# Hybrid decoder layer on one Trainium2 core: another order of three engines' queues around a seven-product output projection

## The chip, the cores and the metric

The kernel is written in Bass and runs on 1 core of one Trainium2 chip, in one launch. The metric is the device time in microseconds (us). A profile is one execution of the program recorded by the hardware profiler; its own time and its span stand beside each other below.

## What is computed

One layer of a hybrid decoder for 512 tokens of width 1024, all in float32. A combined input projection feeds two token mixers (a gated linear recurrence and a top-k sparse attention). Each mixer's output is projected up to width 1024, the two are weighted by sigmoid gates and added (`merged`). What the change touches is the end:

```python
merged = jax.nn.sigmoid(ga) * ua + jax.nn.sigmoid(gb) * ub      # (512, 1024)
y = jnp.einsum('bld,de->ble', merged, w_out)                    # (512, 1024) x (1024, 1024)
return layer_norm(ALPHA * x + y, ln_g, ln_b)                    # over the 1024 columns of a row
```

## The kernel before, in words

**Every float32 product is three products.** ACT rounds an operand to a high part (`hi`), POOL or DVE subtracts to get the low part (`lo = raw - hi`), and PE adds hi*hi, hi*lo and lo*hi into one PSUM bank. The input projection and the two up projections run as 31 "units" of weights (`UNITS`, 256 columns each), each in 4 quarters, so there are 124 steps `q`. SP loads the units, ACT makes their high parts, POOL their low parts, PE multiplies. Beside that the mixers' work is placed by hand: each engine has a function `side(q)`, and tables such as `OUT_HI_AT`, `OUT_LO_AT` and `T1_AT` say at which q an engine does what. A step q is only a place in an engine's queue, each engine runs its queue strictly in order, and semaphores tie the engines together.

**The up projections** are the last four units, `up0` to `up3`, q = 108 to 123: 16 fills of a bank with 12 matmuls each (`quarter_up`), over four banks. `merge(m)` on DVE, m = 0 to 7 (before line L1719), reads two fills, frees their banks with its first two instructions (L1711, L1712), adds them to `mix` (L1715), and after ACT has rounded it (`round_merged`, L1196) subtracts the low part (L1718), which is what PE needs as operand m of the output projection. After an odd m, `sum_rows` (L1728 to L1735) makes four sums and differences, `round_sums` (ACT, L1201) and `sum_rows_lo` (DVE, L1741) their high and low parts. The last merge (m = 7) and what follows it stand behind the loop over q.

**The output projection** multiplies a 2x2 block matrix (halves of the 512 rows; even and odd tiles of 128 of the inner dimension against halves of the columns) with seven products of half-size blocks in place of eight (a Strassen-like scheme). PE takes them in the order `OUT_WEIGHTS` = b11, b21, t1, t2, b22, t3, t4, and each for i = 0 and 1 (128 rows each), 12 matmuls of 128x128 by 128x512 for each of these 14: 168 matmuls (L958, L960, L961). Sums: b11 and b21 give the rows 0 to 255, columns 0 to 511 (bank `c11`). b11 alone is also kept aside by ACT (`keep_first`, L1222, into `first_sum`), because b21 is added into the same bank: b21 waits for `first_kept`. The common sum U = b11 + t2 goes into the three other blocks. The weights b11, b12, b21, b22 come from HBM; t1 to t4 are their differences, made by DVE (`sum_out`, L1762, 128x2048 elements each; t1 at q = `T1_AT`). Their high parts are made by ACT (`split_out_hi`, L1217, two halves each), their low parts by POOL (`split_out_lo`, L2044, four pieces each, in the order 0, 1, 4, 3, 5, 6 of `OUT_WEIGHTS`), that of t1 by DVE (`first_sum_lo`, L1768).

**Behind the last merge** ACT's queue before is: the last `round_merged`, the last `round_sums`, a load of the table of functions (L1346), the two halves of `split_out_hi(4)`, `keep_first` for i = 0 and 1, the splits 3, 5, 6, then the layer norm's small steps. DVE's queue is: last merge, `sum_rows`, t2, `sum_rows_lo`, t3, `rows_11(0)`, t4, `rows_11(1)`, `rows_12` for both i, `late_residuals` for both i, statistics of b22's rows, `rows_22` for both i, statistics of t4's rows. In `rows_12` (L1793 to L1795) DVE makes U (`u_sum`) and V = c12 + U (`v_sum`) in SBUF and puts V plus ALPHA*x back into bank `c12`, on which b22 is added by PE (wait on `pre_12`). `late_residuals` (L1779 by way of `with_residual`) adds ALPHA*x of the rows 256 to 511 to U and V in SBUF. `rows_22` (L1808, L1809) combines them with t3 and frees t4 (`pre_21`):

```python
def rows_22(i):
    t = 2 + i
    wait_y_full(dve, "t3", i)
    nc.vector.tensor_tensor(y_sb[:, t, 512:], c21_bank[i][:], y_sb[:, t, 512:], ALU.add).then_inc(dve_step, 1)
    nc.vector.tensor_tensor(c21_bank[i][:], c21_bank[i][:], y_sb[:, t, 0:512], ALU.add).then_inc(pre_21, 1)
```

**The layer norm** works on 4 tiles of 128 rows (t) in two halves of 512 columns. DVE takes statistics (L1771) and aggregates (L1774); ACT takes the root (`root`). The scaling is done in one of two ways: on DVE with two instructions (`normalise_half`, L1819, L1822), or on ACT and POOL (`shift` and `scale_rows` on ACT, then `scale_columns` with two instructions on POOL, L2050, L2052). `ON_POOL` lists for each t the halves that take the second way: before it is both halves of t = 0 and 1, and half 1 of t = 2, five in all. SP stores each half in the order of t as soon as it is done (L626).

Of the kernel before, what the change touches and what calls it, by code (L numbers as in the profile page):

```python
# [29 lines left out]
ALU = mybir.AluOpType  # L30
# [64 lines left out]
OUT_HI_AT = {110: (0, 0), 111: (0, 1), 118: (1, 0), 119: (1, 1), 121: (2, 0), 122: (2, 1)}  # L95
OUT_LO_AT = {110: ((0, 0),), 111: ((0, 1),), 114: ((0, 2),), 115: ((0, 3),), 118: ((1, 0),), 119: ((1, 1),),
             120: ((1, 2),), 121: ((1, 3),)}
T1_AT = 116
ON_POOL = ((0, 1), (0, 1), (1,), ())
# [16 lines left out]
def hybrid_kernel(nc, x_t, x_tok, w_units, w_kiwi, b_cols, b_ia, b_vb, lb_cols, g_cols, rel_bias,  # L116
                  ln_g, ln_b, one_hot, ident, causal, tree_masks, out):
    with ExitStack() as ctx:
# [75 lines left out]
        with ExitStack() as s:  # L194
# [13 lines left out]
            with ExitStack() as s2:  # L208
                v_sum = sb("v_sum", [P, 2, SEQ], stack=s2)
# [92 lines left out]
        first_kept, pre_12, pre_21 = sem("first_kept"), sem("pre_12"), sem("pre_21")  # L302
        y_full, y_aggr = sem("y_full"), sem("y_aggr")
# [211 lines left out]
        def row_source(t, half):  # L515

            if half == 1 and t < 2:
                return c12_bank[t][:]
            if half == 0 and t >= 2:
                return c21_bank[t - 2][:]  # L520
            return y_sb[:, t, half * 512:half * 512 + 512]
# [109 lines left out]
        def _(pe):  # L631
# [302 lines left out]
            for n, i in OUT_ORDER:  # L934
                name = OUT_WEIGHTS[n]
                bank, (b_hi, b_lo) = out_banks[name][i], out_weights(n)
                first = name in ("b11", "t1", "t2", "t3")
# [4 lines left out]
                elif name == "t1":  # L942
                    pe.wait_ge(proj_out[i], NPROJ[NMAIN])
                elif name in ("t2", "t3"):
                    pe.wait_ge(up_out[i + 2 * (name == "t3")], 2 * KT // 4)
                elif name == "b22":
                    pe.wait_ge(pre_12, i + 1)
                else:
                    pe.wait_ge(pre_21, i + 1)
# [17 lines left out]
        def _(act):  # L967
# [255 lines left out]

            def root(t):
# [5 lines left out]

            def shift(t):
# [3 lines left out]
                act.wait_ge(ln_shift, 2 * t + 1)  # L1235
                nc.scalar.activation(rstd[:, t, 3:4], rstd[:, t, 2:3], ACT.Copy,
                                     scale=rstd[:, t, 1:2]).then_inc(ln_shift, 1)
                act.wait_ge(ln_shift, 2 * t + 2)
# [63 lines left out]
            for q in range(4 * NMAIN):  # L1302
# [13 lines left out]
                if q in OUT_HI_AT:  # L1316
                    split_out_hi(*OUT_HI_AT[q])
# [22 lines left out]
                if m is not None:  # L1340
                    round_merged(m)
                    if m % 2:
                        round_sums(m // 2)
            round_merged(KT - 1)
            round_sums(PAIRS - 1)
            nc.scalar.preload_act_table_set("natural_log_exp_and_others")  # L1346
            for half in range(2):
                split_out_hi(4, half)
            for i in range(2):
                keep_first(i)  # L1350
            for n in (3, 5, 6):
                for half in range(2):
                    split_out_hi(n, half)
            for t in range(TB):
                root(t)
                if t < TB - 1:
# [6 lines left out]
        def _(dve):  # L1363
# [412 lines left out]
            def with_residual(t, half, other):  # L1776

                c = slice(half * 512, half * 512 + 512)
                link(nc.vector.scalar_tensor_tensor(out=y_sb[:, t, c], in0=y_sb[:, t, c], scalar=ALPHA, in1=other,  # L1779
                                                    op0=ALU.mult, op1=ALU.add))  # L1780

            def rows_11(i):
# [3 lines left out]
                with_residual(i, 0, c11_bank[i][:])  # L1786
                row_stats(i, 0)

            def rows_12(i):
# [3 lines left out]
                link(nc.vector.tensor_tensor(u_sum[:, i, :], m6_bank[i][:], first_sum[:, i, :], ALU.add))  # L1793
                link(nc.vector.tensor_tensor(v_sum[:, i, :], c12_bank[i][:], u_sum[:, i, :], ALU.add))
                nc.vector.scalar_tensor_tensor(out=c12_bank[i][:], in0=y_sb[:, i, 512:], scalar=ALPHA,  # L1795
                                               in1=v_sum[:, i, :], op0=ALU.mult, op1=ALU.add).then_inc(pre_12, 1)

            def late_residuals(i):

                dve.wait_ge(res_in[2 + i], 16)  # L1800
                with_residual(2 + i, 0, u_sum[:, i, :])
# [333 lines left out]
```

## Time and profile before

| what | value |
|---|---|
| median of 3 runs | 476.32 us (475.74 to 476.94) |
| the profiled execution, its own time | 476.05 us |
| its span | 474.2 us |
| PE busy | 448.2 us, 95% of the span |
| DVE, ACT, POOL busy | 320.1, 237.7, 194.8 us |
| mean granted clock of PE | 0.976 |

The span is what the trace covers; 1.85 us of the execution's own time lie around it. Engines are PE (matmul), PEld (its weight loads), DVE, ACT, POOL and SP (which issues the DMAs). A row of a timeline gives start and duration in us, the engine, the line of the kernel, the operation, output<-inputs with their sizes, how many are merged into the row, and in brackets how long the engine was idle before it and who ended that. In the rows, high parts of the b weights are `x_hi`, `w_hi` or `w_late`, low parts `x_lo` or `w_lo`, as they lie in buffers that are used again; `z_a`, `z_b` and `w_raw` hold the raw weights.

### The profile page before, as it was taken

What the parts mean: (1) busy time and instruction counts of PE and PEld (TensorE: products, weight loads), DVE (VectorE), ACT (ScalarE), POOL (GpSimd) and SP (SyncE); (2) the same over time, 40 slices, a digit from 0 to 9 for tenths busy, and PEclk for the clock granted to TensorE, in tenths of its full rate; (3) what the DMA queues carried; (4) which work ended last, traced back from release to release, by engine and by line L of the source; (5) the groups of instructions that cost most, each with busy time, mean ns of one, the idle gap of its engine ahead of it and who ended that gap; (6) DMA issues with size and microseconds to landing.
All of it is one profiled execution on the core that took longest, in us unless ns stands there. A gap on an engine that the chain in (4) does not pass through costs nothing.

```text
span 474.2 us, 7699 instructions
## 1 busy us (share of the span) xinstructions
PE 448.2 (95%) x2946; PEld 364.9 (77%) x2946; DVE 320.1 (68%) x581; ACT 237.7 (50%) x401; POOL 194.8 (41%) x179
## 2 busy tenths in 40 slices
PE   8999999999999999999999999999999998929990
PEld 7778888888888788888878878878888876717770
DVE  4535699999999643458899958806300678895685
ACT  5734554442457625658685658347743224345050
POOL 0444444490667607540040000000655775409956
PEclk9999999999999999999999999999999998978996
DMA  8818202274026600222202220320464520420003
GB/s 260 276 42 311 75 25 83 92 183 169 0 91 156 201 1 2 88 90 88 91 2 91 91 90 1 107 74 1 140 219 173 177 89 4 171 91 1 0 27 151
DMA packets 16724, 47.73 MB, mean 101 GB/s; under 512 B 2440, under 2 KB 4272, under 8 KB 16176
## 3 DMA queue, kind: packets, MB, share of 16 engines
q1 hardware_dynamic: 16448, 47.05, 30.0%
q8 instruction: 23, 0.38, 0.3%
q10 hardware_dynamic: 240, 0.20, 0.2%
q14 instruction: 13, 0.11, 0.1%
HBM read 43.04 MB, written 2.11 MB: 95 GB/s over the span
## 4 chain that ended last, share of the span: by engine, by line
PE 82%; DVE 7%; POOL 4%; ACT 3%; issue 2%; DMA 1%; POOLq 0%; DVEq 0%; ACTq 0%
PE bank L633 20%; PE bank L634 20%; PE bank L635 20%; PE bank L794 2%; PE bank L779 2%; PE bank L877 2%; PE bank L830 2%; POOL y_sb L2050 1%; PE bank L958 1%; PE bank L960 1%; PE bank L961 1%; POOL y_sb L2052 1%; PE bank L770 1%; PE bank L769 1%; DVE y_sb L1779 1%
## 5 line engine op out<-in xcount | busy, mean ns | idle before, releaser
L1970 POOL TENSOR_TENSOR w_lo<-w_raw,w_hi 128x512 fp32r<-128x512 f32 x84 | 112.7, 1368 | 161.8 <-ACT w_hi L969 161.8
L633 PE MATMUL bank<-x_hi,w_hi 128*128 128x512 f32 x336 | 133.0, 396 | 0.0
L634 PE MATMUL bank<-x_lo,w_hi 128*128 128x512 f32 x336 | 131.2, 390 | 0.0
L635 PE MATMUL bank<-x_hi,w_lo 128*128 128x512 f32 x336 | 130.9, 390 | 0.0
L633 PEld LDWEIGHTS bank<-x_hi,w_hi 128*128 128x128 f32 x336 | 63.1, 188 | 13.8 <-issue 0.8
L635 PEld LDWEIGHTS bank<-x_hi,w_lo 128*128 128x128 f32 x336 | 63.1, 188 | 13.6
L634 PEld LDWEIGHTS bank<-x_lo,w_hi 128*128 128x128 f32 x336 | 63.1, 188 | 12.2
L969 ACT ACTIVATE w_hi<-w_raw 128x1024 fp32r<-128x1024 f32 (+2 forms) x63 | 62.4, 1011 | 5.8 <-PE bank L635 3.3
L1056 ACT ACTIVATE prob<-prob,nmax 128x128 f32<-128x128 f32 (+3 forms) x32 | 17.7, 555 | 41.6 <-DVE nmax L1497 41.5
L633 PE MATMUL bank<-o_hi,w_hi 128*128 128x512 f32 x64 | 25.5, 399 | 2.3 <-DVE mix L1711 2.3
L1473 DVE MAX8 best<-score 128x8 f32<-128x256 f32 (+2 forms) x48 | 26.8, 558 | 1.0
L1485 DVE COPY prob_t<-bank 128x128 f32<-128x128 f32 (+3 forms) x32 | 14.3, 486 | 19.0 <-PE bank L779 18.9
L1474 DVE MATCH_REPLACE8 score<-best,score 128x256 f32<-128x256 f32 (+2 forms) x48 | 26.0, 542 | 0.0
L634 PE MATMUL bank<-o_lo,w_hi 128*128 128x512 f32 x64 | 25.6, 400 | 0.0
L635 PE MATMUL bank<-o_hi,w_lo 128*128 128x512 f32 x64 | 25.6, 400 | 0.0
L633 PE MATMUL bank<-w_hi,x_hi 128*128 128x512 f32 x64 | 25.3, 395 | 0.0
L635 PE MATMUL bank<-w_hi,x_lo 128*128 128x512 f32 x64 | 25.0, 390 | 0.0
L634 PE MATMUL bank<-w_lo,x_hi 128*128 128x512 f32 x64 | 24.9, 390 | 0.0
L1711 DVE TENSOR_TENSOR mix<-bank,gate_a_hi 128x512 f32<-128x512 f32 x4 | 2.7, 686 | 31.7 <-PE bank L635 31.7
L1988 POOL TENSOR_TENSOR logit<-t,pen 128x256 f32<-128x256 f32 x24 | 17.4, 738 | 9.1 <-DVE nmax L1497 9.1
L1046 ACT ACTIVATE relus<-bank 128x256 f32<-128x256 f32 (+2 forms) x24 | 10.5, 489 | 21.0 <-PE bank L759 21.0
L1463 DVE SCALAR_TENSOR_TENSOR score<-relus,w_idx,score 128x256 f32<-128x256 f32 (+2 forms) x21 | 15.6, 744 | 7.7 <-ACT relus L1046 6.0
(274 smaller groups left out, 855.4 us busy)
## 6 DMA issues: line engine op xcount, KB each, us to landing
w_raw<-in_w_units SPq DMA_DIRECT2D x58, 512.0 KB, 4.7
w_raw<-in_w_units SPq DMA_DIRECT2D x2, 1024.0 KB, 4.8
y_sb<-in_x_tok SPq DMA_DIRECT2D x4, 512.0 KB, 5.2
out<-y_sb SPq DMA_DIRECT2D x8, 256.0 KB, 2.0
x_raw_hi<-in_x_t SPq DMA_DIRECT2D x4, 256.0 KB, 4.7
x_raw_lo<-in_x_t SPq DMA_DIRECT2D x4, 256.0 KB, 6.6
t_turned<-t_row SPq DMA_DIRECT2D x1, 1024.0 KB, 9.6
q_hi_g<-q_hi_g SPq DMA_DIRECT2D x8, 128.0 KB, 4.0
```

The source lines that it names most:

```text
L633: nc.tensor.matmul(dst, a_hi, b_hi, start=first, stop=False)
L634: nc.tensor.matmul(dst, a_hi, b_lo, start=False, stop=False)
L635: return nc.tensor.matmul(dst, a_lo, b_hi, start=False, stop=last)
L969: nc.scalar.activation(split_target(u, kiwi_hi, x_hi, w_hi)[:, k, :], raw(u)[:, k, :], ACT.Copy).then_inc(done, 1)
L1046: nc.scalar.activation(relus[:, i % 2, 0:n], log_bank[i % 2][:, 0:n], ACT.Relu, scale=QSCALE).then_inc(log_out[i % 2], 1)
L1056: nc.scalar.activation(prob[:, i % 4, 0:n], prob[:, i % 4, 0:n], ACT.Exp, bias=nmax[:, i % 4:i % 4 + 1], scale=-1.0, accum_out=prob_sum[:, ...
L1463: ins = nc.vector.scalar_tensor_tensor(out=score[b][:], in0=relus[:, i % 2, 0:n], scalar=w, in1=score[b][:], op0=ALU.mult, op1=ALU.add)
L1473: link(nc.vector.max(best8[:], score[b][:]))
L1474: link(nc.vector.match_replace(score[b][:], best8[:], score[b][:], TAKEN))
L1485: nc.vector.tensor_copy(prob_t[:, i % 4, 0:n], turn_bank[i % 2][:, 0:n]).then_inc(turn_out[i % 2], 1)
L1970: nc.gpsimd.tensor_tensor(split_target(u, kiwi_lo, x_lo, w_lo)[:, k, :], raw(u)[:, k, :], split_target(u, kiwi_hi, x_hi, w_hi)[:, k, :].bi ...
L1988: nc.gpsimd.tensor_tensor(logit[:, i % 2, n - band:n], t5[:, h, 2 * P - band:], pen[b][:, n - band:] if b else causal_sb[:], ALU.add).then ...
```

## The change

ACT's and POOL's work on the weights b11, b21, t1 moves to other steps, t1 itself one step earlier; the table load moves from behind the last `round_sums` to q = 109; `split_out_hi(4)` goes ahead of the last `round_merged`, and `keep_first` right behind `round_merged` and `round_sums`. DVE adds ALPHA*x to bank `c12` before t2 is done (`early_rows`), and U by one instruction afterwards; `v_sum` and `late_residuals` go. ACT copies U into bank `c21` (`move_u`), t3 is added onto it by PE. Rows stay in their PSUM banks up to the normalisation's second instruction. `ON_POOL` has two halves left in place of five; DVE takes six in place of three.

```diff
--- before.py
+++ after.py
@@ -92,11 +92,10 @@
 LO_DVE = tuple(range(Q_PREP[0] // 4 + 1, Q_MERGE // 4 + 2))
-OUT_HI_AT = {110: (0, 0), 111: (0, 1), 118: (1, 0), 119: (1, 1), 121: (2, 0), 122: (2, 1)}
-OUT_LO_AT = {110: ((0, 0),), 111: ((0, 1),), 114: ((0, 2),), 115: ((0, 3),), 118: ((1, 0),), 119: ((1, 1),),
-             120: ((1, 2),), 121: ((1, 3),)}
-T1_AT = 116
-ON_POOL = ((0, 1), (0, 1), (1,), ())
+OUT_HI_AT = {109: ((0, 0),), 110: ((0, 1),), 117: ((1, 0),), 118: ((1, 1),), 120: ((2, 0), (2, 1))}
+OUT_LO_AT = {110: 0, 119: 1}
+T1_AT, T1_LO_AT = 115, 121
+ON_POOL = ((), (1,), (1,), ())
 ROUNDS = TOPK // 8
@@ -300,6 +297,7 @@
         first_kept, pre_12, pre_21 = sem("first_kept"), sem("pre_12"), sem("pre_21")
+        u_done, u_moved, early_12 = sem("u_done"), sem("u_moved"), sem("early_12")
         y_full, y_aggr = sem("y_full"), sem("y_aggr")
@@ -514,11 +512,7 @@
-            if half == 1 and t < 2:
-                return c12_bank[t][:]
-            if half == 0 and t >= 2:
-                return c21_bank[t - 2][:]
-            return y_sb[:, t, half * 512:half * 512 + 512]
+            return ((c11_bank, c12_bank), (c21_bank, m6_bank))[t // 2][half][t % 2][:]
@@ -934,15 +928,17 @@
                 bank, (b_hi, b_lo) = out_banks[name][i], out_weights(n)
-                first = name in ("b11", "t1", "t2", "t3")
+                first = name in ("b11", "t1", "t2")
                 if name == "b11":
...
                     pe.wait_ge(proj_out[i], NPROJ[NMAIN])
-                elif name in ("t2", "t3"):
-                    pe.wait_ge(up_out[i + 2 * (name == "t3")], 2 * KT // 4)
+                elif name == "t2":
+                    pe.wait_ge(up_out[i], 2 * KT // 4)
+                elif name == "t3":
+                    pe.wait_ge(u_moved, i + 1)
                 elif name == "b22":
@@ -1221,6 +1217,12 @@
+            def move_u(i):
+
+                act.wait_ge(up_out[2 + i], 2 * KT // 4)
+                act.wait_ge(u_done, i + 1)
+                nc.scalar.activation(c21_bank[i][:], u_sum[:, i, :], ACT.Copy).then_inc(u_moved, 1)
+
             def root(t):
@@ -1228,14 +1230,17 @@
+            def shifted(t):
+                return sum(bool(halves) for halves in ON_POOL[:t])
+
             def shift(t):
...
                 act.wait_ge(ln_rstd, t + 1)
-                act.wait_ge(ln_shift, 2 * t + 1)
+                act.wait_ge(ln_shift, 2 * shifted(t) + 1)
                 nc.scalar.activation(rstd[:, t, 3:4], rstd[:, t, 2:3], ACT.Copy,
                                      scale=rstd[:, t, 1:2]).then_inc(ln_shift, 1)
-                act.wait_ge(ln_shift, 2 * t + 2)
+                act.wait_ge(ln_shift, 2 * shifted(t) + 2)
@@ -1313,8 +1318,10 @@
                         split_hi(v, q - hi_quarter(v))
-                if q in OUT_HI_AT:
-                    split_out_hi(*OUT_HI_AT[q])
+                for n, half in OUT_HI_AT.get(q, ()):
+                    split_out_hi(n, half)
+                if q == 109:
+                    nc.scalar.preload_act_table_set("natural_log_exp_and_others")
                 if q == Q_ITEM[0] - 2:
@@ -1341,19 +1348,20 @@
                         round_sums(m // 2)
+            split_out_hi(4, 0)
+            split_out_hi(4, 1)
             round_merged(KT - 1)
+            keep_first(0)
             round_sums(PAIRS - 1)
-            nc.scalar.preload_act_table_set("natural_log_exp_and_others")
-            for half in range(2):
-                split_out_hi(4, half)
-            for i in range(2):
-                keep_first(i)
+            keep_first(1)
             for n in (3, 5, 6):
...
                     split_out_hi(n, half)
+            for i in range(2):
+                move_u(i)
             for t in range(TB):
                 root(t)
-                if t < TB - 1:
+                if ON_POOL[t]:
                     shift(t)
@@ -1773,54 +1781,59 @@
-            def with_residual(t, half, other):
+            def with_residual(dst, t, half, other):
                 c = slice(half * 512, half * 512 + 512)
-                link(nc.vector.scalar_tensor_tensor(out=y_sb[:, t, c], in0=y_sb[:, t, c], scalar=ALPHA, in1=other,
-                                                    op0=ALU.mult, op1=ALU.add))
+                return nc.vector.scalar_tensor_tensor(out=dst, in0=y_sb[:, t, c], scalar=ALPHA, in1=other,
+                                                      op0=ALU.mult, op1=ALU.add)
...
                 dve.wait_ge(res_in[i], 16)
-                with_residual(i, 0, c11_bank[i][:])
+                link(with_residual(c11_bank[i][:], i, 0, c11_bank[i][:]))
                 row_stats(i, 0)
+
+            def early_rows(i):
+
+                wait_y_full(dve, "t1", i)
+                dve.wait_ge(res_in[2 + i], 16)
+                link(with_residual(y_sb[:, 2 + i, 512:], 2 + i, 1, c12_bank[i][:]))
+                with_residual(c12_bank[i][:], i, 1, c12_bank[i][:]).then_inc(early_12, 1)
...
                 dve.wait_ge(first_kept, i + 1)
-                link(nc.vector.tensor_tensor(u_sum[:, i, :], m6_bank[i][:], first_sum[:, i, :], ALU.add))
-                link(nc.vector.tensor_tensor(v_sum[:, i, :], c12_bank[i][:], u_sum[:, i, :], ALU.add))
-                nc.vector.scalar_tensor_tensor(out=c12_bank[i][:], in0=y_sb[:, i, 512:], scalar=ALPHA,
-                                               in1=v_sum[:, i, :], op0=ALU.mult, op1=ALU.add).then_inc(pre_12, 1)
-
-            def late_residuals(i):
-
-                dve.wait_ge(res_in[2 + i], 16)
-                with_residual(2 + i, 0, u_sum[:, i, :])
-                with_residual(2 + i, 1, v_sum[:, i, :])
+                nc.vector.tensor_tensor(u_sum[:, i, :], m6_bank[i][:], first_sum[:, i, :], ALU.add).then_inc(u_done, 1)
+                dve.wait_ge(u_done, i + 1)
+                dve.wait_ge(early_12, i + 1)
+                nc.vector.tensor_tensor(c12_bank[i][:], c12_bank[i][:], u_sum[:, i, :], ALU.add).then_inc(pre_12, 1)
...
                 wait_y_full(dve, "t3", i)
-                nc.vector.tensor_tensor(y_sb[:, t, 512:], c21_bank[i][:], y_sb[:, t, 512:], ALU.add).then_inc(dve_step, 1)
-                nc.vector.tensor_tensor(c21_bank[i][:], c21_bank[i][:], y_sb[:, t, 0:512], ALU.add).then_inc(pre_21, 1)
-                steps[0] += 1
-                dve.wait_ge(dve_step, steps[0])
+                link(nc.vector.tensor_tensor(m6_bank[i][:], c21_bank[i][:], y_sb[:, t, 512:], ALU.add))
+                with_residual(c21_bank[i][:], t, 0, c21_bank[i][:]).then_inc(pre_21, 1)
                 row_stats(t, 1)
...
                 c = slice(half * 512, half * 512 + 512)
-                y = y_sb[:, t, c]
+                y = row_source(t, half)
                 dve.wait_ge(y_aggr, t + 1)
-                link(nc.vector.scalar_tensor_tensor(out=y, in0=row_source(t, half), scalar=aggr[:, t, 0:1],
+                link(nc.vector.scalar_tensor_tensor(out=y, in0=y, scalar=aggr[:, t, 0:1],
                                                     in1=ln_gb[:, 0, c], op0=ALU.subtract, op1=ALU.mult))
                 dve.wait_ge(ln_rstd, t + 1)
-                nc.vector.scalar_tensor_tensor(out=y, in0=y, scalar=rstd[:, t, 1:2], in1=ln_gb[:, 1, c],
+                nc.vector.scalar_tensor_tensor(out=y_sb[:, t, c], in0=y, scalar=rstd[:, t, 1:2], in1=ln_gb[:, 1, c],
                                                op0=ALU.mult, op1=ALU.add).then_inc(y_done[t][half], 1)
+
+            def normalise(t):
+
+                for half in range(2):
+                    if half not in ON_POOL[t]:
+                        normalise_half(t, half)
@@ -1902,7 +1915,7 @@
                         sum_rows_lo(m // 2 - 1)
-                if q == T1_AT + 6:
+                if q == T1_LO_AT:
                     first_sum_lo()
@@ -1935,23 +1948,24 @@
             rows_11(1)
+            early_rows(0)
+            early_rows(1)
             rows_12(0)
             rows_12(1)
-            late_residuals(0)
-            late_residuals(1)
             for t in range(2):
...
                 aggregate(t)
+                if t == 0:
+                    normalise(0)
             rows_22(0)
             rows_22(1)
+            normalise(1)
             for t in (2, 3):
...
                 aggregate(t)
-                for half in range(2):
-                    if half not in ON_POOL[t]:
-                        normalise_half(t, half)
+                normalise(t)
@@ -2053,8 +2067,9 @@
                 side(q)
-                for n, piece in OUT_LO_AT.get(q, ()):
-                    split_out_lo(n, piece)
+                if q in OUT_LO_AT:
+                    for piece in range(4):
+                        split_out_lo(OUT_LO_AT[q], piece)
             for n in LO_ORDER[2:]:
```

## Rows read from the trace of the kernel before

**Rows 1.** The page: PE's busy time, and the chain that ended last, by engine

```profile
PE 448.2 (95%) x2946; PEld 364.9 (77%) x2946; DVE 320.1 (68%) x581; ACT 237.7 (50%) x401; POOL 194.8 (41%) x179
PE 82%; DVE 7%; POOL 4%; ACT 3%; issue 2%; DMA 1%; POOLq 0%; DVEq 0%; ACTq 0%
```

**Rows 2.** Windows of PE: length, busy (matmuls), granted clock, DMA share, GB/s

```profile
392.90:396.60 3.70, 3.69 (x9) 0.55 0.02 4
413.10:414.10 1.00, 0.08 (x1) 1.00 1.02 401
427.10:430.80 3.70, 3.62 (x9) 0.50 0.00 0
```

**Rows 3.** Timeline of PE, last third of the up projections and the output projection

```profile
392.91 0.53 PE L633 MATMUL bank<-o_hi,w_hi 128*128 128x512 f32 x1 [2.28 <-DVE mix L1711]
396.66 0.39 PE L633 MATMUL bank<-o_hi,w_hi 128*128 128x512 f32 x1
...
410.98 0.39 PE L958 MATMUL bank<-x_hi,even_hi 128*128 128x512 f32 x1
...
414.11 0.50 PE L958 MATMUL bank<-x_hi,even_hi 128*128 128x512 f32 x1 [0.93 <-DVE even_lo L1718]
...
427.18 0.80 PE L958 MATMUL bank<-x_hi,odd_hi 128*128 128x512 f32 x1 [9.35 <-ACT first_sum L1222]
...
451.16 0.39 PE L958 MATMUL bank<-x_hi,s_hi_hi 128*128 128x512 f32 x1
...
461.81 0.39 PE L961 MATMUL bank<-x_hi,odd_lo 128*128 128x512 f32 x1
```

**Rows 4.** Timeline of ACT around the up projections' start and the last merge

```profile
372.05 0.42 ACT L1196 ACTIVATE even_hi<-mix 128x256 fp32r<-128x256 f32 x1 [5.05 <-DVE mix L1715]
...
419.43 0.63 ACT L1196 ACTIVATE odd_hi<-mix 128x512 fp32r<-128x512 f32 x1 [5.82 <-DVE mix L1715]
...
423.35 1.28 ACT L1346 ACT_TABLE_LOAD   x1
424.64 2.00 ACT L1217 ACTIVATE w_late<-w_raw 128x1024 fp32r<-128x1024 f32 x2
426.55 1.06 ACT L1222 ACTIVATE first_sum<-bank 128x512 f32<-128x512 f32 x2
```

**Rows 5.** Timeline of DVE over the same stretch and the tail

```profile
389.36 2.90 DVE L1762 TENSOR_TENSOR z_a<-z_b,z_a 128x2048 f32<-128x2048 f32 x1 [2.89 <-POOL x_lo L2044]
392.18 0.68 DVE L1711 TENSOR_TENSOR mix<-bank,gate_a_hi 128x512 f32<-128x512 f32 x1
...
413.63 0.42 DVE L1718 TENSOR_TENSOR even_lo<-mix,even_hi 128x256 fp32r<-128x256 f32 x1 [1.33 <-ACT even_hi L1196]
...
415.11 2.28 DVE L1768 TENSOR_TENSOR w_lo<-z_a,w_hi 128x2048 fp32r<-128x2048 f32 x1
...
433.40 2.67 DVE L1762 TENSOR_TENSOR w_raw<-w_raw,z_a 128x2048 f32<-128x2048 f32 x1
435.99 0.68 DVE L1779 SCALAR_TENSOR_TENSOR y_sb<-y_sb,bank 128x512 f32<-128x512 f32 x1
...
446.94 1.30 DVE L1795 SCALAR_TENSOR_TENSOR bank<-y_sb,v_sum 128x512 f32<-128x512 f32 x1
448.15 1.77 DVE L1779 SCALAR_TENSOR_TENSOR y_sb<-y_sb,u_sum 128x512 f32<-128x512 f32 x1
...
453.12 0.70 DVE L1771 BATCH_NORM_STATS2 stats<-bank 128x6 f32<-128x512 f32 x1
...
460.57 0.75 DVE L1819 SCALAR_TENSOR_TENSOR y_sb<-bank,aggr,ln_gb 128x512 f32<-128x512 f32 x1
```

**Rows 6.** Timeline of POOL: a split beside DVE's wide subtraction, the last scaling

```profile
432.63 7.10 POOL L2044 TENSOR_TENSOR w_lo<-z_a,w_hi 128x512 fp32r<-128x512 f32 x4
...
468.92 1.59 POOL L2052 TENSOR_TENSOR y_sb<-y_sb,ln_gb 128x512 f32<-128x512 f32 x1
```

**Rows 7.** The store DMAs: issues (duration ns min/median/max, first and last start us)

```profile
L626 SPq DMA_DIRECT2D out<-y_sb x8: 332/341/454, 458.8 to 471.4; - x8
```

More of the change, by code:

```diff
@@ L207, in hybrid_kernel @@
             g_b_1 = sb("g_b_1", [P, 4, SEQ], stack=s)
-            with ExitStack() as s2:
-                v_sum = sb("v_sum", [P, 2, SEQ], stack=s2)
             mix = sb("mix", [P, 2, SEQ], stack=s)
```

## The prediction

> **What bounds the kernel now.** I read the page first: PE is busy for 95% of the span and is 82% of the chain that ended last, and the chain leaves PE only near the end [rows 1]. So what counts is where PE stands still and what lies behind its last product. The timeline of PE gives three gaps in the stretch that the change touches, each with its releaser, and a tail [rows 3]. PE waits 2.28 us before 392.91 for DVE's third merge; 0.93 us before 414.11 for the low part of operand 6; 9.35 us before 427.18 for ACT's copy `first_sum`. Its last product starts at 461.81 and takes 0.39, so it ends at 462.2, and the span ends at 474.2: a tail of 12.0 us without PE. The windows add a cost that a gap has behind it: after the gap of 2.28 and after that of 9.35 the granted clock is 0.55 and 0.50, the lower of the two levels (1.2 GHz), for nine matmuls each; around the gap of 0.93 it stays at 1.00 (2.4 GHz) [rows 2]. The pace at the higher level is (461.81 - 451.16)/47 = 0.227 us a matmul; the nine slow ones took 396.66 - 392.91 = 3.75 instead of 2.04, so one fall of the clock costs 1.7 us [rows 3].
>
> **Term 1: t1 and the gap of 2.28.** DVE stood idle for 2.89 us before t1 (389.36) until POOL had b11's last low parts [rows 5]. These now come at q = 110, right behind up1's part; t1 moves one step earlier in DVE's queue, with the same neighbours. So t1 can start at 389.36 - 2.89 = 386.5. It costs 2.28 (the subtraction of that width with POOL idle) to 2.90 (beside POOL) [rows 5]. POOL is released at about the same moment for up3, so I take nearly the upper end: the third merge starts at 389.3 instead of 392.18. It frees PE's bank 0.7 later, at 390.0, before PE wants it (392.91 - 2.28 = 390.6). The gap and its slow matmuls go; the 72 matmuls left of the up projections end at 390.5 + 72 x 0.227 = 406.8, against 410.98 [rows 3]: 4.2 us earlier.
> The trace shows the same width at 2.28 and 2.90, and a 128x512 operation with two SBUF inputs at 1.77 beside POOL [rows 5]. The Trainium skill (SBUF - State Buffer, "Who interferes with whom") says that a VectorE instruction with two SBUF inputs and a GpSimd one that reads SBUF exclude each other, the first to start holding the port throughout. By that rule with t1 first, merge 3 comes 0.6 us sooner and the total is 461.6; with POOL first it is what I take.
>
> **Term 2: that gain is mostly not PE's.** From merge 3 to the low part of operand 6 DVE's chain took 413.63 + 0.42 - 392.18 = 21.9 us [rows 5]. The change adds to it: ACT does both halves of b21's high part ahead of operand 4 instead of one (+1.0, half of the 2.00 for two [rows 4]); `first_sum_lo`, 2.2 us [rows 5], now stands ahead of merge 6 instead of behind. It saves 0.7 of the 1.33 that DVE waited for operand 6 [rows 5], since t1's high parts no longer stand ahead of that rounding (0.42 remain, plus a hand-over). Sum 24.4: operand 6 is ready at 389.3 + 24.4 = 413.7, against 414.05. PE reaches it at 406.8 + 9 x 0.227 = 408.9, about 0.6 later if merge 5 (12 us behind merge 3) frees its bank late. So b11 gets **a new gap of 4 to 5 us**, longer than the one with a clock fall [rows 2, 3], and I charge 1.7: b11's other 15 matmuls end at 413.7 + 3.4 + 1.7 = 418.8.
>
> **Term 3: the gap of 9.35.** It was ACT's queue: rounding of operand 7 at 419.43, sums, table load 1.28, two splits 2.00, then the copies [rows 4]. Now the splits are ahead of the rounding (they need b22 and up3's end, both past by 413.7), the table load is at q = 109, where ACT idles 5.05 us before 372.05 [rows 4] and hides 1.28 and the moved first half of b11 (1.0); without that cover it would cost 1.3. Operand 7 follows operand 6 by 3.9 us (s_lo 1.1, merge and rounding 2.8, as from 417.3 to 420.06), the copy takes 0.55 (1.06 for two): first copy at 418.1, before b11 ends. The second stands behind `round_sums`, at 420.9; b21's second half wants it at 418.8 + 2.7 = 421.5. No wait: b21 starts at 418.8 instead of 427.18.
>
> **Term 4: from b21 to the end of PE.** Before it took 462.2 - 427.18 = 35.0, with one clock fall: 33.3 without. Can the others follow? DVE's queue from its last sums (419.7): t2 2.2, low part 1.1, t3 2.2, rows_11 1.4, t4 2.67, rows_11 1.4, early_rows 2 x 1.4, U and its addition 1.4, by 0.68 for each add, 0.70 for each statistic and 2.28 to 2.67 for the wide ones [rows 5]: 434.9, up to 1.2 later beside POOL. PE is there at 418.8 + 6 x 2.72 = 435.1. Wait of 0 to 0.9 at b22; I take 0.3. `move_u` (0.55 each) runs on an idle ACT about 4 us before t3; `rows_22` needs 1.4 per i and has 2.7. POOL: b22's low parts 414.5 to 421.6, t2's from 423.2 (its high part) to 430.3 by the slow 7.10 for four [rows 6]; PE wants the last at 431.8. Covered by 1.5. PE ends at 418.8 + 33.3 + 0.3 = 452.4: **9.8 us earlier**.
>
> **Term 5: the tail.** Before, POOL's backlog of ten scalings ended at 470.51 [rows 6] and the last store was issued at 471.4 [rows 7], 2.8 before the span's end. Now tile 0 is normalised under t3, tile 1 and half of tile 2 under t4, and DVE, 0.7 late at the last product, does statistics 0.7, aggregate 0.2, and four instructions of at most 0.75 plus 0.04 between them [rows 5] = 3.2: 4.8 behind PE; with the store's 2.8 the tail is 7.6 instead of 12.0: **4.4 us less**. ACT's and POOL's half of tile 2 ends about 1 us before that. No store but the last is on the path.
> The second normalising instruction with a bank as input isn't in the trace: 0.75 (its neighbour [rows 5]) at the low end, 1.30 (two SBUF inputs, a bank as output, beside POOL [rows 5]) at the high end. It has one SBUF input like the 0.75, so I take that.
> The add with a bank as input took 0.68 [rows 5]. The Trainium skill (VectorE: DVE Perf Modes, "The TRN2 errata") speaks against this change here: 120 + FD cycles from PSUM, 58 + FD from SBUF, which is 65 ns more for each of the operations that now stay in banks. By that rule the tail's four would add 0.3 us (462.5); the row shows no such surplus.
>
> **Sum.** 474.2 - 9.8 - 4.4 = 460.0 span, plus the 1.85 around it = 461.9 for an execution like the profiled one (476.05), which lies 0.3 under the median of the runs: 462.2.
>
> **Rivals.**
> (a) The sum above, 460.5 to 464: chance 0.60.
> (b) DVE becomes the bound: operations that write or read banks cost 1.30 instead of 0.68 to 0.75. Five of them lie between t4 and b22 (+2.8, less the 0.2 of slack), four in the tail (+2.2): +4.8, 467.0, or 465.5 with half in the first part. For it the 1.30 row; against it that the same form beside an idle POOL is never so slow. 0.14.
> (c) Less is lost in front: no clock fall behind b11's gap, or t1 first and less contention. Then b11 ends 1.7 sooner but waits 1.0 for the copy; with merge 3 at 388.7 all of it 0.6 sooner: 460.3 to 461.5. 0.13.
> (d) POOL's low parts of t2 arrive after PE wants them, since DVE's wide subtractions now run beside them. If both fours cost 2 us more than 7.1: +2.5, 464.7. 0.08.
> (e) Slower: the clock. PE comes out of b11's new gap at the lower level and stays there. Ahead of it are 15 + 144 = 159 matmuls at 0.2 more each. Nine are charged; the gain of 14.1 is gone once 70 more are slow, and if all 150 are, the time is 462.2 + 30 = 492. Against it, both falls in the trace ended after nine matmuls [rows 2]. 0.03.
> (f) The change doesn't do what it says: ACT, now with b22's split ahead of operand 7's rounding, stands at the load of b22, everything behind it waits, and b21 starts as late as before; some 10 us come back, and with (b) in the tail nothing is left: 475. The load would have to land 13 us late. 0.02.
>
> A measurement of this kernel can tell 0.3%, 1.4 us, from no change. (a) to (d) are faster by more, 0.95; (f) is the same, 0.02; (e) slower, 0.03. The range holds (a), (c), most of (b) and (d): 459.8 to 466.
>
> **What would show it.** Right: no gap before fill 10; a gap of 4 to 5 us inside b11 released by DVE `even_lo`, with a window at half clock behind it; b21 starts about 419 with no `first_sum` gap; PE ends at 452 and the span about 7.6 later, the last instruction being DVE's. Wrong: a gap at b21 or over 1 us at b22 or t2; statistics or normalising instructions over 1 us; t1 still waiting for POOL; a slow window longer than 4 us.

## The result, and the profile after

The changed kernel takes 463.86 us (463.53 to 463.86, 4 runs), the one before 476.22 us (475.74 to 476.94): a ratio of 0.9737, 95% interval 0.9721 to 0.9754, 12.4 us less. The forecast was 462.2, in a range of 459.8 to 466. In the profiled execution the span is 461.9 us against 474.2. Times of the experiments below are medians of 4 or 5 runs, each with the ratio to the kernel before on the same chip. The variant that came out fastest had one execution of 2539 us among its five: its ratio leaves that one out, its median of 461.18 does not (the other four have 460.97), and the cause was not looked for.

The timeline of PE after the change, every gap in the stretch (they answer to [rows 3]) and its last product:

```profile
403.04 0.50 PE L627 MATMUL bank<-o_hi,w_hi 128*128 128x512 f32 x1 [0.85 <-DVE mix L1719]
413.65 0.80 PE L954 MATMUL bank<-x_hi,even_hi 128*128 128x512 f32 x1 [2.83 <-DVE even_lo L1726]
423.54 0.50 PE L954 MATMUL bank<-x_hi,odd_hi 128*128 128x512 f32 x1 [0.62 <-ACT first_sum L1218]
434.47 0.50 PE L954 MATMUL bank<-w_hi,s_hi_lo 128*128 128x512 f32 x1 [0.27 <-POOL w_lo L2058]
454.10 0.39 PE L957 MATMUL bank<-x_hi,odd_lo 128*128 128x512 f32 x1
```

The gaps of 2.28 and 9.35 us are gone; four small ones, 4.6 us in all, stand for 12.6. PE ends at 454.5 instead of 462.2, and the tail behind it is 461.9 - 454.5 = 7.4 instead of 12.0. So of the 12.3 us of span, 7.7 came ahead of PE's end and 4.6 behind it. (This execution runs 0.43 behind that of before already at merge 0, DVE's first `mix` at 369.34 against 368.91, well ahead of anything that moved; differences below are given with that in mind, and it is called the offset.)

ACT around the last merge (to be read against [rows 4]):

```profile
417.69 0.63 ACT L1192 ACTIVATE odd_hi<-mix 128x512 fp32r<-128x512 f32 x1 [2.66 <-DVE mix L1723]
418.23 0.58 ACT L1218 ACTIVATE first_sum<-bank 128x512 f32<-128x512 f32 x1
421.94 1.06 ACT L1197 ACTIVATE s_hi_lo<-s_raw 128x1024 fp32r<-128x1024 f32 x1 [3.13 <-DVE s_raw L1743]
422.91 0.58 ACT L1218 ACTIVATE first_sum<-bank 128x512 f32<-128x512 f32 x1
```

The first copy of b11 follows the rounding at once; the second one waits 3.13 us for DVE's sums, and b21's second half waits for it. DVE after the change (against [rows 5]):

```profile
386.98 3.37 DVE L1770 TENSOR_TENSOR z_a<-z_b,z_a 128x2048 f32<-128x2048 f32 x1
390.27 0.68 DVE L1719 TENSOR_TENSOR mix<-bank,gate_a_hi 128x512 f32<-128x512 f32 x1
...
413.17 0.43 DVE L1726 TENSOR_TENSOR even_lo<-mix,even_hi 128x256 fp32r<-128x256 f32 x1 [0.48 <-ACT even_hi L1192]
...
416.03 1.63 DVE L1723 TENSOR_TENSOR mix<-mix,g_b 128x512 f32<-128x512 f32 x1
418.36 0.99 DVE L1726 TENSOR_TENSOR odd_lo<-mix,odd_hi 128x512 fp32r<-128x512 f32 x1 [0.70 <-ACT odd_hi L1192]
419.27 1.50 DVE L1736 TENSOR_TENSOR s_raw<-mix 128x256 f32<-128x256 f32 x1
...
456.08 0.76 DVE L1826 SCALAR_TENSOR_TENSOR bank<-bank,aggr,ln_gb 128x512 f32<-128x512 f32 x1
...
458.33 0.75 DVE L1829 SCALAR_TENSOR_TENSOR y_sb<-bank,rstd,ln_gb 128x512 f32<-128x512 f32 x1
```

and POOL (against [rows 6]):

```profile
414.16 6.33 POOL L2058 TENSOR_TENSOR w_late<-w_raw,w_late 128x512 fp32r<-128x512 f32 x4 [7.68 <-ACT w_late L1213]
425.29 9.13 POOL L2058 TENSOR_TENSOR w_lo<-z_a,w_hi 128x512 fp32r<-128x512 f32 x4 [4.79 <-ACT w_hi L1213]
434.38 5.03 POOL L2058 TENSOR_TENSOR x_lo<-z_b,x_hi 128x512 fp32r<-128x512 f32 x4
```

The reader is to see three things. In DVE's last merge and the first sum behind it the forms with two SBUF inputs take 1.63, 0.99 and 1.50 us where they take 0.69, 0.69 and 0.42 alone, and that is the stretch 414.2 to 420.5 in which POOL, which idled there before, makes b22's low parts. POOL's four pieces of t2 take 9.13 us, those of t3 5.03. And the normalising instructions with a bank as input take 0.75.

### The profile page after: what moved, and what is told of

It is laid out like the page before. It is cut to its first block, busy times and chain, and to the rows that moved or that the text cites. A ratio compares the mean times of both kernels' runs of the same rounds, so it can differ in the third digit from the quotient of the medians.

```text
span 461.9 us, 7700 instructions
## 1 busy us (share of the span) xinstructions
PE 448.9 (97%) x2946; PEld 365.5 (79%) x2946; DVE 319.4 (69%) x585; ACT 236.7 (51%) x398; POOL 185.3 (40%) x173
## 4 chain that ended last, share of the span: by engine, by line
PE 84%; DVE 9%; POOL 2%; issue 2%; ACT 2%; DVEq 0%; POOLq 0%
PE bank L627 21%; PE bank L628 21%; PE bank L629 20%; PE bank L788 2%; PE bank L773 2%; POOL w_lo L2058 2%; PE bank L871 2%; PE bank L824 2%; DVE s_lo L1749 1%; DVE z_a L1770 1%; DVE mix L1723 1%; PE bank L764 1%; PE bank L763 1%; PE bank L954 1%; PE bank L957 1%
```

## The experiments

**ACT's last part alone, on the kernel before.**

```diff
+                if q == 109:
+                    nc.scalar.preload_act_table_set("natural_log_exp_and_others")
...
+            split_out_hi(4, 0)
+            split_out_hi(4, 1)
             round_merged(KT - 1)
+            keep_first(0)
             round_sums(PAIRS - 1)
-            nc.scalar.preload_act_table_set("natural_log_exp_and_others")
-            for half in range(2):
-                split_out_hi(4, half)
-            for i in range(2):
-                keep_first(i)
+            keep_first(1)
```

> The kernel before with ACT's last part alone changed (table load at q = 109, b22's split ahead of the last rounding, the copies of b11 right behind the rounding and the sums). Theory (the gap of 9.35 us was ACT's order): the first copy ends near 420.6 instead of 427.1, b21 starts 6.6 us earlier, with a gap of about 2.9 us and one fall of the clock as before; tail of 12 us unchanged: 469.7 us. Rival (DVE's and POOL's backlog takes the place of ACT's): b21 starts early, but PE waits at t2 or b22, and less than 3 us come out: over 473 us.

Measured: 473.41 us, ratio 0.9942 (0.9927 to 0.9957): 2.8 us, not 6.6. The timelines of PE, DVE and POOL say where the rest stayed:

```profile
423.15 0.53 PE L958 MATMUL bank<-x_hi,odd_hi 128*128 128x512 f32 x1 [4.79 <-ACT first_sum L1222]
```

```profile
415.67 3.38 DVE L1769 TENSOR_TENSOR w_lo<-z_a,w_hi 128x2048 fp32r<-128x2048 f32 x1
420.35 1.60 DVE L1716 TENSOR_TENSOR mix<-mix,g_b 128x512 f32<-128x512 f32 x1
```

```profile
415.18 7.90 POOL L2045 TENSOR_TENSOR w_late<-w_raw,w_late 128x512 fp32r<-128x512 f32 x4 [5.72 <-ACT w_late L1217]
```

ACT was ready, but operand 7's rounding began at 421.99 instead of 419.43 (0.56 of it the offset of this execution), because the early split let POOL begin beside DVE's last wide subtraction (3.38 instead of 2.28) and merge (1.60 instead of 0.69). The rival's number held, not its mechanism: PE's small waits at b22 and t4 are 0.59 and 0.26. The tail was not unchanged either: PE ends at 459.40 in a span of 472.1, so it is 12.7 us.

**The same part undone, on the changed kernel** (order of ACT's queue: rounding, sums, b22's split, both copies; the table load stays at q = 109).

> The changed kernel with the two copies of b11 and b22's split put back behind the last sums on ACT; everything else as changed. Theory: b21's first half starts near 425.5 instead of 420.0, and a second fall of the clock costs 1.7 to 3: 471 to 473 us. Rival (b21's start does not decide, the low parts of t2 on POOL do): under 467 us.

Measured: 466.81 us, ratio 0.9807 (0.9790 to 0.9823), 3 us over the changed kernel; both theories missed (471 to 473, under 467 for the wrong reason).

```profile
422.35 0.79 PE L954 MATMUL bank<-x_hi,odd_hi 128*128 128x512 f32 x1 [5.75 <-ACT first_sum L1218]
```

```profile
415.29 0.69 DVE L1723 TENSOR_TENSOR mix<-mix,g_b 128x512 f32<-128x512 f32 x1
```

b21 starts at 422.35, not 425.5. With b22's split late, POOL idles until 420.95 and DVE's last merge runs at its own pace (0.69): the same coupling from the other side. The run takes back two things at once (the copies and b22's split), so the 3 us are not the price of the copies alone. That gave theory C below.

**Five halves of rows on POOL, as before.** `ON_POOL = ((0, 1), (0, 1), (1,), ())`.

> The changed kernel with five halves of rows scaled on POOL as before, in place of two. Theory (the tail got shorter because the rows' other work on DVE is done ahead, so that POOL could start early anyway): POOL starts its ten operations near 444.4, when t4's low parts are done, ends about 457.8, DVE's last two halves end the kernel as now: 463 to 464 us. Rival (the tail's 4.6 us come from taking three halves off POOL): 467.5 to 468.5 us.

Measured: 462.55 us, ratio 0.9717 (0.9702 to 0.9731): not slower but 1 us faster than the change (463.55 us and 0.9732 when it was run again, below). The intervals of the two ratios overlap; what speaks for a difference is that all four runs here (462.46 to 462.89) lie under all four there (463.31 to 463.66, on another chip), and the tail in the profiles.

```profile
453.66 0.39 PE L957 MATMUL bank<-x_hi,odd_lo 128*128 128x512 f32 x1
```

```profile
443.90 1.31 POOL L2064 TENSOR_TENSOR y_sb<-y_sb,ln_gb 128x512 f32<-128x512 f32 x1
...
455.71 1.26 POOL L2066 TENSOR_TENSOR y_sb<-y_sb,ln_gb 128x512 f32<-128x512 f32 x1
```

POOL starts its scalings at 443.90, as soon as t4's low parts are made, where before it started at 456.09; it is done at 457.0, DVE at 458.1. The tail is 460.7 - 454.05 = 6.65 us, 0.8 shorter than the change's, since DVE is free when the last product ends. The edit changes nothing but `ON_POOL`, so taking halves off POOL did not shorten the tail.

**The steps of the weights' parts as before** (`OUT_HI_AT`, `OUT_LO_AT`, `T1_AT` as in the kernel before, `first_sum_lo` at q = 122).

> The changed kernel with the steps of b11's, b21's and t1's parts and of t1 itself as before. Theory A (moving them only moves PE's wait, the chain on DVE decides): the gap of 2.3 us in the up projections is back with its fall of the clock, the gap in b11 is 1 us again, and one of 2.9 us stands before b21; time within 1 us of the changed kernel, 463 to 465 us. Theory B (the steps are worth the 2.2 us by which operand 7 comes sooner and a fall of the clock): 466 to 468 us.

Measured: 466.78 us, ratio 0.9805 (0.9790 to 0.9819): theory B by the time, the steps are worth 3 us. What theory A said of the first gap came true in part: it is back, but no fall of the clock follows it in this profile, and the gap in b11 is 2.49 us, not 1.

```profile
392.79 0.50 PE L628 MATMUL bank<-o_hi,w_hi 128*128 128x512 f32 x1 [2.29 <-DVE mix L1720]
414.00 0.50 PE L955 MATMUL bank<-x_hi,even_hi 128*128 128x512 f32 x1 [2.49 <-DVE even_lo L1727]
422.48 0.80 PE L955 MATMUL bank<-x_hi,odd_hi 128*128 128x512 f32 x1 [4.79 <-ACT first_sum L1219]
```

With the offsets taken off, operand 6 is 0.9 us later than in the change (PE goes on at 414.00 against 413.65, in an execution that is 0.56 ahead at merge 0). The rest is lost behind it, on DVE:

```profile
414.99 3.38 DVE L1777 TENSOR_TENSOR w_lo<-z_a,w_hi 128x2048 fp32r<-128x2048 f32 x1
419.68 1.60 DVE L1724 TENSOR_TENSOR mix<-mix,g_b 128x512 f32<-128x512 f32 x1
```

`first_sum_lo` stands ahead of merge 7 again, beside POOL's parts of b22 (414.51 to 422.41). The old steps with b22's parts moved away were not run, so how much of the 3 us is the order and how much the meeting with POOL is not shown.

**The change again, and three edits beside it.** In the first edit POOL makes b22's low parts behind t2's:

```diff
-        LO_ORDER = (0, 1, 4, 3, 5, 6)
+        LO_ORDER = (0, 1, 3, 4, 5, 6)
```

In the second PE gets twelve products more (`FILL = 12`) ahead of b11's last pair, so that it works through the gap:

```diff
+                        if name == "b11" and j == 3:
+                            pe.wait_ge(proj_out[0], NPROJ[NMAIN])
+                            for _ in range(FILL):
+                                nc.tensor.matmul(c12_bank[0][:], a_hi, b_hi[:, 2, :], start=True, stop=True)
```

The third is everything on the rows alone: the changed kernel with steps, ACT's last part, table load and `ON_POOL` as before.

> The changed kernel once more, beside the next three on one chip: 463.9 us by either theory, within 0.5.

> The changed kernel with one edit: POOL makes b22's low parts behind t2's instead of ahead of them. Theory C (the early split of b22 put POOL's work beside DVE's last merge, whose operations with two SBUF inputs then took 1.0 to 1.6 us instead of 0.4 to 0.7; that is why b11's second copy came at 423.5 and not at 421): DVE's last merge and sums take 2.3 us less, b21's second half starts 2 us sooner, POOL starts t2's low parts 2 us sooner, 461.9 us. Rival (DVE's pace there does not set PE's, or b22's low parts come too late): 463.5 us or more.

> The changed kernel with twelve products more (into a bank not yet in use, thrown away) ahead of b11's last pair, so that PE works through most of the gap. Theory C: the fall of the clock goes, b11 ends up to 3 us sooner, but b21's second half waits for ACT's second copy as before: 463.9 us, within 0.5. Rival (the fall of the clock, three us in this profile, is what made my forecast too low): 461 to 462 us.

> Everything of the change on the rows alone (early residuals, U copied into c21, rows kept in their banks, the normalisation of tiles 0 and 1 ahead of t3's and t4's rows), with the steps, ACT's last part, the table load and the halves on POOL as before. If the parts add up, the steps being worth 2.9 and ACT's part 3.0 and the halves on POOL -1.3: 468.5 us. If ACT's part and the steps each pay only with the other (two gaps in a row on one chain): 466 or 471 us. The tail by this theory is as in the run with five halves on POOL, 6.7 us behind PE's last product.

| kernel | us | ratio (interval) |
|---|---|---|
| the change again | 463.55 | 0.9732 (0.9719 to 0.9745) |
| b22's low parts behind t2's | 461.18 | 0.9679 (0.9666 to 0.9692) |
| gap in b11 filled | 463.32 | 0.9729 (0.9716 to 0.9742) |
| the rows' part alone | 470.40 | 0.9875 (0.9859 to 0.9890) |

The first edit bears theory C out: 2.4 us less than the change by the medians (2.6 without the long execution), 2.0 expected. ACT, DVE and POOL of that kernel:

```profile
419.69 0.58 ACT L1218 ACTIVATE first_sum<-bank 128x512 f32<-128x512 f32 x1
```

```profile
415.15 0.69 DVE L1723 TENSOR_TENSOR mix<-mix,g_b 128x512 f32<-128x512 f32 x1
416.54 0.69 DVE L1726 TENSOR_TENSOR odd_lo<-mix,odd_hi 128x512 fp32r<-128x512 f32 x1 [0.69 <-ACT odd_hi L1192]
417.14 0.42 DVE L1736 TENSOR_TENSOR s_raw<-mix 128x256 f32<-128x256 f32 x1
```

```profile
422.07 9.15 POOL L2058 TENSOR_TENSOR w_lo<-z_a,w_hi 128x512 fp32r<-128x512 f32 x4 [16.48 <-ACT w_hi L1213]
431.18 5.05 POOL L2058 TENSOR_TENSOR w_late<-w_raw,w_late 128x512 fp32r<-128x512 f32 x4
```

The second copy starts at 419.69 instead of 422.91 (0.9 of which is this execution's own lead), b21 doesn't wait for it at all, and PE ends at 451.3. PE's last product:

```profile
450.91 0.39 PE L957 MATMUL bank<-x_hi,odd_lo 128*128 128x512 f32 x1
```

The filled gap was to show what the fall of the clock costs. The windows of PE over the gap, filled (first) and in the change run again (second):

```profile
410.20:413.20 3.00, 2.92 (x13) 1.00 1.01 385
```

```profile
410.50:413.30 2.80, 0.00 (x0) 1.00 0.93 334
413.30:418.50 5.20, 3.70 (x15) 1.00 0.42 161
```

The time did not move. It could hardly have: the clock did not fall in the change run again either, after the same gap of 2.83 us (the granted clock is 1.00 behind it), while in the first profile of the change 14 matmuls behind that gap are at the lower level and in the run with five halves on POOL eight. So the filled gap says nothing of the fall's price. The two profiles of the same kernel do. Their spans are 461.9 with the fall and 461.6 without, but the one with the fall was already 0.35 late at merge 0 and behind the gap (413.65 against 413.30), and it is 0.33 late when PE ends (454.49 against 454.16): the fall took nothing. Without it b11 ends sooner, and PE waits 1.53 and 1.65 us for ACT's two copies instead of 0 and 0.62.

The rows' part alone brings 6.0 us, the largest share; the 468.5 us of parts that add up was 2 too low, and the 471 of parts that pay only together is nearer. PE's end is that of before (462.6 against 462.2), the tail 469.2 - 462.6 = 6.6 us:

```profile
462.23 0.39 PE L958 MATMUL bank<-x_hi,odd_lo 128*128 128x512 f32 x1
```

```profile
452.00 1.29 POOL L2064 TENSOR_TENSOR y_sb<-y_sb,ln_gb 128x512 f32<-128x512 f32 x1 [2.26 <-ACT y_sb L1249]
```

POOL starts at 452.0 for 456.09, because DVE takes the statistics of b22's rows when they are there, and not behind four late residuals [rows 5]. A second thing changed in the tail, and the run doesn't separate the two. In the kernel before, the normalising instructions on DVE whose rows lie in SBUF have two SBUF inputs and run beside POOL's scalings; with the rows in banks they have one. The last two before, and in the rows' part alone:

```profile
465.97 1.75 DVE L1819 SCALAR_TENSOR_TENSOR y_sb<-y_sb,aggr,ln_gb 128x512 f32<-128x512 f32 x1
467.75 1.63 DVE L1822 SCALAR_TENSOR_TENSOR y_sb<-y_sb,rstd,ln_gb 128x512 f32<-128x512 f32 x1
```

```profile
465.09 0.75 DVE L1826 SCALAR_TENSOR_TENSOR bank<-bank,aggr,ln_gb 128x512 f32<-128x512 f32 x1
465.88 0.75 DVE L1829 SCALAR_TENSOR_TENSOR y_sb<-bank,rstd,ln_gb 128x512 f32<-128x512 f32 x1
```

DVE is done 7.2 us behind PE's end before (469.38) and 4.0 behind it here (466.63), where it, and not POOL (465.50), ends the kernel.

**Can both better ways be had?** The first of two attempts takes b22's low parts behind t2's and five halves on POOL; the second, in addition, t1's low parts on POOL (`LO_ORDER = (0, 1, 2, 3, 4, 5, 6)`, at q = 121) in place of `first_sum_lo`.

> The changed kernel with b22's low parts behind t2's (461.2 us in the last comparison) and five halves of rows on POOL (1.0 to 1.3 us less than two halves, since DVE is then free when the last product ends). If the two are independent: 460.0 us, 459.7 to 460.4. Rival (POOL's t4 parts now end 1.5 us later against PE, and push its scalings to the end): 461 us or more.

> As best1, and t1's low parts (2.28 us on DVE ahead of merge 6) made by POOL, which idles from 405.6 to 422 in the run with b22's parts moved. Theory C (POOL beside DVE's operations with two SBUF inputs costs DVE as much as it saves): DVE's sums, merge 6 and low parts take about 2 us more beside POOL, 459.7 to 460.4 as best1. Rival (2.28 us off DVE's chain is a gain): 458 us.

Measured: 464.94 us, ratio 0.9762 (0.9749 to 0.9775), and 467.10 us, ratio 0.9809 (0.9796 to 0.9822). Both are slower than the change: in the first the rival's number and its reason held, and both numbers on the second missed. POOL in the first:

```profile
446.96 1.29 POOL L2064 TENSOR_TENSOR y_sb<-y_sb,ln_gb 128x512 f32<-128x512 f32 x1
...
458.65 1.26 POOL L2066 TENSOR_TENSOR y_sb<-y_sb,ln_gb 128x512 f32<-128x512 f32 x1
```

PE ends at 452.1, but POOL's ten scalings begin at 446.96 and end at 459.91, 2.9 later than in the run with five halves alone, and three stores queue behind them: POOL has become what ends last. It idled 16.48 us ahead of t2's parts and lacks them at the end. In the second, DVE beside POOL's extra 6.00 us:

```profile
406.61 1.51 DVE L1733 TENSOR_TENSOR s_raw<-mix 128x256 f32<-128x256 f32 x1
408.04 1.51 DVE L1734 TENSOR_TENSOR s_raw<-mix 128x256 f32<-128x256 f32 x1
409.47 1.50 DVE L1737 TENSOR_TENSOR s_raw<-s_raw,mix 128x256 f32<-128x256 f32 x1
```

Each of four sums (the fourth took 1.37) waits out a piece of POOL's: 5.89 us for 1.67, 4.2 more for 2.28 saved, and the gap in b11 grows to 4.85.

**Two small parts of the change undone.** The early residuals behind U (`early_rows(i)` called in `rows_12` between U and its addition), and the table load behind the last `round_sums`.

> The changed kernel with the residuals of the second column half not folded in ahead of t2's end but behind U, as part of the work between t2 and b22. Theory (DVE's queue is full there, the work only moves inside it, and PE waited none at b22): the chain from t2's first half to b22's permission gets 1.4 us longer and b22 waits 0.2 to 0.7: 463.8 to 464.3 us. Rival (the early fold is worth its four operations of 0.69): 466 us.

> The changed kernel with the table load of 1.28 us behind the last rounding of sums instead of at q = 109. Theory: it delays ACT's second copy of b11, for which PE waits 0.6 to 1.7, and t2's high parts by the part that the wait for DVE's t2 (0.66) doesn't cover: 464.2 to 464.9 us. Rival (ACT has room there): 463.6 us.

Measured: 463.70 us, ratio 0.9738 (0.9724 to 0.9751), no difference from the change's 0.9732; and 465.57 us, ratio 0.9773 (0.9760 to 0.9786), 2 us over the change and 0.7 over the theory's upper end. PE in each:

```profile
437.92 0.50 PE L954 MATMUL bank<-w_late,s_hi_hi 128*128 128x512 f32 x1 [0.25 <-DVE bank L1811]
```

```profile
424.53 0.50 PE L954 MATMUL bank<-x_hi,odd_hi 128*128 128x512 f32 x1 [3.06 <-ACT first_sum L1218]
```

b22 waits 0.25 for the late residuals. The table load of 1.28 puts 1.4 us to the wait for the second copy (3.06 for 1.65), all of it on PE's path. Most of the rest is the clock in this profile: behind this longer gap eight matmuls are at the lower level, the first whole one being

```profile
426.18 0.63 PE L954 MATMUL bank<-x_hi,odd_hi 128*128 128x512 f32 x1
```

and here no wait follows at once that could hide them. From the end of the wait to PE's end it is 31.8 us (424.53 to 456.37), in the change run again 31.0 (423.20 to 454.16), the 0.27 us of waiting for t2's parts counted in there.

## Why the prediction came out where it did

The total was right, 1.7 us too low, and the likeliest case (a) is the one that happened. By its terms:

**Term 1 (t1) held** in its place: t1 starts at 386.98 without a wait and the gap of 2.28 is gone. It took 3.37 us, over my upper end of 2.90, so merge 3 began at 390.27 for 389.3 (0.4 of it the offset). The rule of the Trainium skill (SBUF - State Buffer, "Who interferes with whom") is borne out: of two neighbours with two SBUF inputs on DVE and an SBUF input on POOL the later waits, and a 128x256 sum of 0.42 takes 1.51 beside a POOL piece of 1.3. In the change POOL's second piece of b22's parts lasts from 415.84 to 417.11, and DVE's addition of merge 7, which starts at 416.03, ends at 417.66, 0.55 behind that. By that rule I should have asked of every moved POOL step what on DVE it would land beside; I asked it of t1 alone.

**Term 2 held**: operand 6 was ready at 413.6 for 413.7, PE waited for it in the middle of b11, 2.83 us and 0.85 at merge 5 instead of 4 to 5 in one. But that the steps therefore bring nothing ahead of b21, as theory A of the fourth experiment drew from it, is wrong: undone, they cost 3 us, and in that run `first_sum_lo` stands ahead of merge 7 and beside POOL.

**The step that failed is in term 3**: "Operand 7 follows operand 6 by 3.9 us", and the second copy "at 420.9". It was 4.7 (413.60 to 418.32, the end of its rounding), and the copy ended at 423.49: 2.6 us late, 1.9 of them between the two copies (4.7 for 2.8), where DVE's low part and first sum took 0.99 and 1.50. I had counted b22's early split on ACT and on POOL's later deadline, but not its low parts on POOL beside DVE's last merge and sums. With them moved away the distance is 3.8 (412.72 to 416.51) and the copy ends at 420.27, 7.55 behind operand 6 where I had 7.2 and the change has 9.9; that run is the price of the slip, 2.4 us (461.18 for 463.55), more than the whole miss.

**Term 4**: PE's end at 454.5 for 452.4, 2.1 late: 0.4 of offset, the rest the late copy, then 0.27 for t2's parts, where I had seen 1.5 of slack. They began at 425.29, not 423.2, and their 9.13 us for my 7.10 goes with the t3 and t4 subtractions beside them. The wait at b22 was none.

**Term 5, right in size, wrong in cause**: a tail of 7.4 for 7.6. I put it down to halves taken off POOL together with the earlier normalisation. Five halves on POOL with the rest of the change give 6.65, and the rows' part alone, with five, 6.6. So the gain lies in the rows' part: DVE's statistics are no longer behind the late residuals, and the normalising instructions are no longer lengthened beside POOL (1.75 and 1.63 before, 0.75 now); how it divides between these two is not shown. Taking three halves off POOL cost 0.8 of it, about the 0.7 by which I had DVE late. The instruction with a bank as input took 0.75, as I chose, and the 1.30 of rival (b) never appeared. The surplus that the Trainium skill gives for PSUM operands (VectorE: DVE Perf Modes, "The TRN2 errata") is not to be seen: DVE's additions with one bank input took 0.68 to 0.70 (`rows_12`, `rows_22`), the same width with both inputs in SBUF 0.69 in the merge above, not 65 ns less.

**The clock**: I charged one fall in b11 at 1.7. It fell in some profiles and not in others after the same gap; where it fell in the change's own profile it cost nothing, since PE otherwise waits 1 to 2 us for the copies right behind. The charge was thus a term too many. Rival (c) prices its absence at 0.7: without it the sum is 461.5 and the miss 2.4, which is the price of term 3's slip. That the total missed by 1.7 only is in so far luck. Rival (c) was true in its first half in some executions, and brought nothing, which its own "waits 1.0 for the copy" had half said; its lower end of 460.3 does not follow from its terms, 462.2 - 0.7 - 0.6 = 460.9. Rivals (b), (e) and (f) showed no trace. (d) showed its beginning, 0.27 us, and its price was summed wrongly: two more us on b22's parts are mostly taken up by POOL's idle time ahead of t2's (421.6 to 423.2), so by its own figures POOL would end 0.9 behind PE, not 2.5.

**The parts don't add up.** Alone on the kernel before: the rows 6.0, ACT's part 2.8. Undone from the change: ACT's part 3.3, the steps 3.2, the halves on POOL -1.0, the table load 2.0, the early fold of the residuals 0.2, within the error. The change whole is 12.8, run again. The steps alone on the kernel before were not run.

Left open: a count of halves on POOL between two and five together with b22's parts behind t2's was not tried. What sets whether the clock falls after a gap of 2.8 us was not looked into.

## What to carry to other kernels

When work is moved earlier on one engine, look at what it releases on the next one, and beside which instructions of a third that will then run; here a split that was ready too early cost 2.4 us through POOL and DVE, and one line of order gave it back (461.18 us, the fastest version seen, 2.4 us under the change). Here an idle stretch of POOL was not free for use while DVE's chain of operations with two SBUF inputs was the critical one: 2.28 us moved off DVE cost 4.2 there. In the tail ask when the first of a backlog can start before asking which engine should do it.

## What was not expected of the hardware

Eight profiles have the gap of 2.8 us in b11 ahead of the same matmuls. 14 matmuls behind it are at the lower clock in one, eight in one, seven in two and none in four. Ahead of the gap these kernels differ in one thing only, the place of the table load, in one of the four without a fall. The gap of 2.3 us in the up projections had nine slow matmuls behind it in the kernel before, and none in the three runs that have it again. And the cost of two engines meeting can exceed the work moved: four DVE sums of 0.42 us took 1.37 to 1.51 each beside POOL pieces.
